# Query projections of latent attention: from one tile per head to one nope tile per pair and one rope tile per two pairs

## The chip, the cores and the metric

One core of a Trainium2 chip runs the whole program. The metric is the device time of one execution in microseconds, as the median of several runs. One more execution was taken by the profiler; its trace has the start and duration of every instruction.

## The reference, cut to what matters

One decoder layer: multi-head latent attention for 1024 prompt tokens and for 8 x 4 sample tokens (these with a paged cache of 4096 positions), then LayerNorm, a gated feed-forward part with a width-3 convolution, LayerNorm. The change touches the query projection and the rotation of queries and keys.

```python
d = x @ w_a_down
c_q = rms_norm(d[..., :384], g_q_norm)                 # Q_LORA
c_kv = rms_norm(d[..., 384:640], g_kv_norm)            # KV_LORA
k_r = d[..., 640:]                                     # 32 rotary columns, one key for all heads
q = (c_q @ w_a_uq).reshape(b, t, 16, 96)               # 16 heads, 64 plain + 32 rotary
x1, x2 = xf[..., :16], xf[..., 16:]                    # apply_rope
rope = concatenate([x1 * cos - x2 * sin, x1 * sin + x2 * cos])
sc = (einsum(q_nope, k_nope) + einsum(q_rope, k_r)) * ATTN_SCALE, causal
o = softmax(sc) @ v
```

## The kernel before, in words

All products are in float32 accuracy: each operand is split into a high part (a rounding to the engine's faster float32r) and a low part (the rest), and each product is three matmuls (hi x hi, hi x lo, lo x hi), `mm3`, lines 728 to 730. The splitting is the work of ScalarE (high, a copy) and VectorE (low, a subtraction).

Stages: `project` (down projection, norms, transposes; to about 98 us), `attend` (prompt attention, 98 to 503 us), `decode` (sample attention with the pages, to about 720 us), `mix`, `ffn`. The heads of `attend` are worked in 8 pairs p. A pair has 16 units n (a query group g of 256 tokens from the last to the first, head hh, half r); wide units come first (scores up to 1024 columns wide), narrow ones (128 to 512) at n = 8 to 15. For every n, TensorE issues in this order: the scores of n + 1, the transposes of the probabilities of n - 1, products with the values (`VALUES_AT`), and pieces of projection work. While pair p is worked on, the projections of pair p + 1 are done, at places written out by hand (`OWN_AT`, `NEXT_AT`): `wt` (a transposed weight), `v0`, `v1` (values), `k0`, `k1` (keys), six query units `q<head><chunk>` with three chunks of CH = 352 tokens, and `t0`, `t1`, `ql` of the pair itself.

The query of one head has 128 rows on the partitions: 64 plain, 32 rotary and 32 rotary with their halves exchanged. The exchange comes from copied weight columns (`split_hi`, on POOL). A table of constants (`rope_query_tab`: the scale, cos, and sin with its sign) is multiplied onto all 128 rows by VectorE (`q_scale`, L1003, tile `q_scaled`, called qf); the keys have the rotary key twice below the plain rows, so that the sum over rows gives x cos + x' sin. ScalarE then makes `q_hi` (`q_high`), VectorE `q_lo` (`q_low`). PSUM has 8 banks: 0 and 1, 2 and 3 hold scores in turn, 4 and 5 transposed probabilities, 6 the output, 7 and free score banks the projections (`BANK`).

Each engine does its instructions in program order. The conditions between them that the text needs:

- scores(n) wait for exp(n - 2) (semaphore `pr`), and for n = 0, 4, 8 for the queries' low parts (`ql_ok`);
- `row_max(n)` (VectorE, `neg_max`, L1018) waits for scores(n), exp(n) (ScalarE, `probs`, L897) for `row_max(n)` and for `inverse(n - 2)` (VectorE, `inv_sums` and `inv_rows`);
- `inverse(n)` waits for exp(n), and stands in VectorE's order behind the projection work of step n + 1;
- at the end of a pair the first scores of the next one wait for `q_scaled` of "q00", since it holds bank 3, and `t0` of the new pair waits for "q10" to leave bank 7.

```python
                    if n == 0 and p:
                        q_high(p, NEXT_AT[NU])
                    if n == 1 and p:
                        inv_copy(p - 1, 0)
```

Of the kernel before, what the change touches and what calls it, by code (L numbers as in the profile page):

```python
# [35 lines left out]
H = 16  # L36
# [54 lines left out]
def rope_tables():  # L91
# [9 lines left out]
    s2 = np.concatenate([-sin, sin], 1).T * np.float32(ATTN_SCALE)  # L101
    plain = np.full((NOPE, TOK), ATTN_SCALE, np.float32)
    query = np.stack([np.concatenate([plain, c2, s2], 0), np.concatenate([c2, s2, plain], 0)], 1)
# [19 lines left out]
def project(nc, io, m, sem):  # L123

    ps = m.ps
    with ExitStack() as ctx:
# [115 lines left out]
        def _(pe):  # L242
# [79 lines left out]
            def early(name):  # L322
# [8 lines left out]
                else:  # L331
                    pe.wait_ge(d_sq, TT - 1)
                    a, b, c, out, hh = m.w.q_halves, (m.cqhi, m.cqlo), slice(0, CH), o[:, 0:CH], int(name[1])
                    sides = [(a[0][:, k, hh, :], a[1][:, k, hh, :], b[0][:, k, c], b[1][:, k, c]) for k in range(KQ)]
# [29 lines left out]
            early("q00")  # L364
            early("q10")
# [76 lines left out]
        def _(dve):  # L442
# [18 lines left out]
            def n_lo_halves(i):  # L461
# [15 lines left out]
            def norm(i):  # L477
# [15 lines left out]
                for at in (DOWN - ROPE, DOWN):  # L493
                    nc.vector.tensor_tensor(nrm[0:r, b, at:at + 16], rt[0:r, 0, :], rt[0:r, 1, :], ALU.subtract)
                    last = nc.vector.tensor_tensor(nrm[0:r, b, at + 16:at + 32], rt[0:r, 2, :], rt[0:r, 3, :], ALU.add)
# [42 lines left out]
FIRST_BANK = {"v0": 0, "k0": 1, "q00": 4, "q10": 5, "wt": 6, "v1": 7, "k1": 2, "q02": 3, "q12": 0, "q01": 4, "q11": 5}  # L538
FIRST_AFTER = {"q12": "v0", "q01": "q00", "q11": "q10"}


class HeadWeights:


    LOADS = 5 * 16

    def __init__(self, tile, stage, sem):
# [7 lines left out]
        self.staged, self.swapped = sem("w_staged"), sem("w_swapped")  # L555
        self.hi_ok, self.lo_ok = sem("w_split_hi"), sem("w_split_lo")

    def load(self, sp, io, p):
        wq = io["w_a_uq"].rearrange("(k p) n -> p k n", p=P)
        for hh, to, n, at in ((0, 0, QK_HEAD, 0), (1, 0, ROPE, QK_HEAD + NOPE), (1, NOPE, NOPE, QK_HEAD)):  # L560
            c = p * 2 * QK_HEAD + at
            sp.dma_start(self.q_staged[:, :, hh, to:to + n], wq[:, :, c:c + n]).then_inc(self.staged, 16)
# [4 lines left out]
    def split_hi(self, nc, pool, p):  # L567

        pool.wait_ge(self.staged, (p + 1) * self.LOADS)
        half, q = ROPE // 2, self.q_staged  # L570
# [1908 lines left out]
```

## Time and profile before

| | us |
|---|---|
| median of 3 runs | 1630.54 (1629.57 to 1631.71) |
| profiled execution | 1627.18 |
| its span, first to last instruction | 1625.3 |
| TensorE busy | 1587.8 |
| VectorE busy | 931.9 |
| ScalarE busy | 586.3 |
| POOL busy | 194.8 |
| one pair of the attention, from the first scores of one (210.56) to those of the next (261.14) | 50.6 |

Busy times are sums of instructions' durations. Matmuls overlap each other in the array, so a matmul's duration (0.32 us for 352 columns) is about twice the distance from its start to the next one's; distances are to be read from starts in the timeline.

### The profile page before, as it was taken

How to read it: one execution, taken by the hardware profiler on the slowest of the kernel's cores; microseconds unless marked ns; L12 is line 12 of the kernel's file. 1: busy time of each engine (PE TensorE's matmuls, PEld its weight loads, DVE VectorE, ACT ScalarE, POOL GpSimd, SP SyncE). 2: the span in 40 equal slices, each digit the busy share in tenths (PEclk: the TensorE clock that was granted, in tenths of full speed). 3: DMA queues.
4: the chain of work that ended last, by engine and by line, in shares of the span. 5: the costliest groups of instructions: out<-in, count | busy, mean ns of one | idle time of the engine just before them, and what ended most of it. 6: DMA issues, size and time to landing. Idle time of an engine off the chain costs nothing. (4 is left out here: it accounts for less than half of the span.)

```text
span 1625.3 us, 29603 instructions
## 1 busy us (share of the span) xinstructions
PE 1587.8 (98%) x10341; PEld 1405.0 (86%) x10341; DVE 931.9 (57%) x1813; ACT 586.3 (36%) x1280; POOL 194.8 (12%) x305
## 2 busy tenths in 40 slices
PE   7989999999999999999999999999999999999997
PEld 6988888888886666657889999999999999999995
DVE  5565666656665555545665465544546455455556
ACT  5455655556553333322233131121312213121145
POOL 1000000000000430000003021120211202112001
PEclk9999999999999999999999999999999999999999
DMA  6111111011113765533123020220202201021003
GB/s 211 54 29 30 28 24 24 13 28 26 23 53 114 237 208 169 167 114 95 39 69 100 27 65 13 65 65 26 65 13 65 64 27 52 25 65 39 13 27 117
DMA packets 151135, 109.18 MB, mean 67 GB/s; under 512 B 54791, under 2 KB 139973, under 8 KB 150904
## 3 DMA queue, kind: packets, MB, share of 16 engines
q1 hardware_dynamic: 148488, 101.76, 21.4%
q0 software_dynamic: 1968, 5.59, 1.2%
q8 instruction: 56, 0.92, 0.2%
q10 hardware_dynamic: 576, 0.52, 0.1%
q14 instruction: 47, 0.39, 0.1%
HBM read 101.88 MB, written 10.14 MB: 69 GB/s over the span
## 5 line engine op out<-in xcount | busy, mean ns | idle before, releaser
L1905 PE MATMUL banks<-act_hi,up_hi 128*128 128x352 f32 (+2 forms) x1040 | 335.6, 323 | 0.7 <-PEq L1497 0.7
L1906 PE MATMUL banks<-act_lo,up_hi 128*128 128x352 f32 (+2 forms) x1040 | 335.1, 322 | 0.0
L1907 PE MATMUL banks<-act_hi,up_lo 128*128 128x352 f32 (+2 forms) x1040 | 334.9, 322 | 0.0
L1905 PEld LDWEIGHTS banks<-act_hi,up_hi 128*128 128x128 f32 x1040 | 195.5, 188 | 1.0 <-issue 0.9
L1906 PEld LDWEIGHTS banks<-act_lo,up_hi 128*128 128x128 f32 x1040 | 195.3, 188 | 0.0
L1907 PEld LDWEIGHTS banks<-act_hi,up_lo 128*128 128x128 f32 x1040 | 195.2, 188 | 0.0
L2204 DVE TENSOR_TENSOR o_t<-o_t,banks 128x352 f32<-128x352 f32 x240 | 120.9, 520 | 94.4 <-PE banks L1907 94.1
L2183 DVE SCALAR_TENSOR_TENSOR conv_out<-conv_in,conv_now,conv_out 128x1072 f32<-128x1072 f32 x42 | 63.9, 1520 | 185.8 <-ACT conv_out L2058 185.8
L1018 DVE TENSOR_REDUCE neg_max<-banks 128x1 f32<-128x896 f32 (+7 forms) x128 | 96.7, 756 | 116.8 <-PE banks L804 116.3
L2049 ACT ACTIVATE conv_in<-banks 128x352 f32<-128x352 f32 x84 | 36.3, 458 | 336.1 <-PE banks L1907 336.1
L1905 PE MATMUL banks<-gated_hi,down_hi 128*128 128x352 f32 x480 | 155.8, 325 | 0.0
L1906 PE MATMUL banks<-gated_lo,down_hi 128*128 128x352 f32 x480 | 154.2, 321 | 0.0
L1907 PE MATMUL banks<-gated_hi,down_lo 128*128 128x352 f32 x480 | 154.1, 321 | 0.0
L897 ACT ACTIVATE probs<-banks,neg_max 128x896 f32<-128x896 f32 (+7 forms) x128 | 94.6, 739 | 43.3 <-DVE inv_rows L1028 23.2
L1905 PEld LDWEIGHTS banks<-gated_hi,down_hi 128*128 128x128 f32 x480 | 90.1, 188 | 1.2
L1906 PEld LDWEIGHTS banks<-gated_lo,down_hi 128*128 128x128 f32 x480 | 90.2, 188 | 0.0
L1907 PEld LDWEIGHTS banks<-gated_hi,down_lo 128*128 128x128 f32 x480 | 90.1, 188 | 0.0
L815 PE MATMUL banks<-ident,probs 128*128 128x128 f32 x576 | 86.9, 276 | 2.5 <-DVE probs_t L1039 2.3
L728 PE MATMUL banks<-k_hi,q_hi 128*128 128x512 f32 (+2 forms) x192 | 71.9, 374 | 8.3 <-DVE q_scaled L1003 6.1
L833 PE MATMUL banks<-probs_t,v_rows 128*64 128x256 f32 (+1 forms) x640 | 72.8, 365 | 0.8 <-DVE probs_t L1039 0.8
L2186 DVE SCALAR_TENSOR_TENSOR conv_out<-conv_in,conv_now,conv_out 128x1072 f32<-128x1072 f32 x42 | 69.3, 1651 | 1.5
L815 PEld LDWEIGHTS banks<-ident,probs 128*128 128x128 f32 x576 | 62.0, 141 | 6.4 <-DVE probs_t L1039 4.3
(340 smaller groups left out, 3085.0 us busy)
## 6 DMA issues: line engine op xcount, KB each, us to landing
weight_stage<-in_w_f_up SPq DMA_DIRECT2D x44, 512.0 KB, 4.8
c_stage<-in_cache_kv_latent SPq DMA_DIRECT2D x140, 128.0 KB, 2.3
down_stage<-in_w_f_down SPq DMA_DIRECT2D x22, 512.0 KB, 4.3
head_weights_stage<-in_cache_kv_latent SPq DMA_DIRECT2D x56, 128.0 KB, 2.2
rope_query_tab<-in_cache_kv_latent SPq DMA_DIRECT2D x56, 128.0 KB, 2.2
o_t<-in_x_prompt SPq DMA_DIRECT2D x8, 512.0 KB, 3.8
rope_rows<-in_cache_k_rope SPq DMA_DIRECT2D x256, 16.0 KB, 2.0
wo_stage<-in_w_a_out POOLq DMA_DIRECT2D x8, 512.0 KB, 4.7
```

Source lines behind the costliest of these rows:

```text
L728: nc.tensor.matmul(o, ws[0], xs[0], start=first, stop=False)
L815: last = nc.tensor.transpose(ps[:, 4 + t % 2, k * P:(k + 1) * P], prob[:, n % 2, c + k * P:c + (k + 1) * P], m.ident[:, :])
L833: last = nc.tensor.matmul(ps[d, 6, q], v[:, j, d], pt[:, g % 2, hh, j, q], start=j == 0, stop=j == 2 * g + 1)
L897: nc.scalar.activation(prob[:, n % 2, 0:wd], src, ACT.Exp, bias=nmax[:, n % 2:n % 2 + 1], accum_out=sums[:, n % 2:n % 2 + 1]).then_inc(pr, 1)
L1018: nc.vector.tensor_reduce(nmax[:, n % 2:n % 2 + 1], src, axis=AXX, op=ALU.max, negate=True).then_inc(nm_ok, 1)
L1905: nc.tensor.matmul(o, ws[0], xs[0], start=first, stop=False)
L1906: nc.tensor.matmul(o, ws[0], xs[1], start=False, stop=False)
L1907: return nc.tensor.matmul(o, ws[1], xs[0], start=False, stop=last)
L2049: nc.scalar.activation(u[i][:, 2 + CH * c:2 + CH * c + CH], src, ACT.Copy).then_inc(ev, 1)
L2183: nc.vector.scalar_tensor_tensor(out=v[i][:, 0:CW], in0=u[i][:, 1:UW - 1], scalar=cwi[:, 1, i, j:j + 1], in1=v[i][:, 0:CW], op0=ALU.mult, ...
L2186: nc.vector.scalar_tensor_tensor(out=v[i][:, 0:CW], in0=u[i][:, 0:UW - 2], scalar=cwi[:, 0, i, j:j + 1], in1=v[i][:, 0:CW], op0=ALU.mult, ...
L2204: nc.vector.tensor_tensor(y, y, ps[:, 4 + unit % 4, 0:CH], ALU.add).then_inc(add, 1)
```

## The change

A pair now has three nope units `n<chunk>` (64 plain rows of both heads, 128 rows together). For every even pair there are also three rope units `r<chunk>` (32 rotary rows of four heads, those of this pair and the next). For an odd pair the rotary rows have been kept in SBUF (`q_raw`, 64 rows) by a ScalarE copy (`rope_saved`). The tile qf now holds both heads of one chunk, instead of two units in turn. ScalarE copies the plain rows out of PSUM with the scale; VectorE makes the rotary rows with four products of 32 rows (cos and sin for each head). The halves are exchanged on the key side: the second copy of the rotary key is written with exchanged halves in `norm`, so the weights need no copied columns, and the table has cos and sin for all rows. `q_high` and `q_low` take both heads at once. For the samples, the sum of the two rotary parts in `m.sr`, before by POOL, is now done with a permuting matmul (`swapped_rope`, last pair, n = 4) and four additions on VectorE (`rope_blocks`, n = 5).

```diff
-s2 = np.concatenate([-sin, sin], 1).T * ATTN_SCALE;  plain = full(ATTN_SCALE)
-query = np.stack([concatenate([plain, c2, s2], 0), concatenate([c2, s2, plain], 0)], 1)
+s2 = np.concatenate([sin, -sin], 1).T * ATTN_SCALE
+query = np.stack([np.tile(c2, (4, 1)), np.tile(s2, (4, 1))], 1)
...
-                    nc.vector.tensor_copy(m.rtnew[:, :], ps[0:2 * ROPE, 7, 3 * P:3 * P + N_SAMPLE])
+                    for b in range(2):
+                        nc.vector.tensor_copy(m.rtnew[b * ROPE:(b + 1) * ROPE, :], ps[0:ROPE, 7, 3 * P:3 * P + N_SAMPLE])
...
-                for at in (DOWN - ROPE, DOWN):
+                for at, swapped in ((DOWN - ROPE, 0), (DOWN, 16)):
...
     def load(self, sp, io, p):
-        for hh, to, n, at in ((0, 0, QK_HEAD, 0), (1, 0, ROPE, QK_HEAD + NOPE), (1, NOPE, NOPE, QK_HEAD)):
+        for h in range(2):
+            c = (2 * p + h) * QK_HEAD
+            sp.dma_start(self.q_staged[:, :, 0, h * NOPE:(h + 1) * NOPE], wq[:, :, c:c + NOPE]).then_inc(self.staged, 16)
+        for h in range(0 if p % 2 else 4):
+            c = (2 * p + h) * QK_HEAD + NOPE
+            sp.dma_start(self.q_staged[:, :, 1, h * ROPE:(h + 1) * ROPE], wq[:, :, c:c + ROPE]).then_inc(self.staged, 16)
     def split_hi(self, nc, pool, p):
-        for hh, rope in ((0, NOPE), (1, 0)):
-            for at, to in ((rope + half, rope + ROPE), (rope, rope + ROPE + half)):
-                last = nc.gpsimd.tensor_copy(q[:, :, hh, to:to + half], q[:, :, hh, at:at + half])
...
+CHUNKS = "210"
+EARLY = [["wt", "v0", "v1", "k1", "r2", "n2", "r1", "n1", "k0", "r0", "n0"], ["wt", "v0", "v1", "k1", "n2", "n1", "k0", "n0"]]
+FIRST = ["v0", "k0", "r0", "n0", "wt", "v1", "k1", "r2", "n2", "r1", "n1"]
-NEXT_AT = {4: "wt", 5: "v0", 6: "v1", 8: "k1", 9: "q02", 10: "q12", 11: "q01", 12: "q11", 14: "k0", 15: "q00", 16: "q10"}
+NEXT_AT = [{4: "wt", 5: "v0", 6: "v1", 8: "k1", 9: "r2", 10: "n2", 11: "r1", 12: "n1", 14: "k0", 15: "r0", 16: "n0"},
+           {4: "wt", 5: "v0", 6: "v1", 8: "k1", 10: "n2", 12: "n1", 14: "k0", 16: "n0"}]
+ROPE_AT = {10: "2", 12: "1", 16: "0"}
+NOPE_AT = {11: "2", 13: "1"}
+LOW_AT = {12: "2", 14: "1"}
...
 PE:  elif name == "t0":
-                    bank_free(p, "q10" if p else "v1")
+                    bank_free(p, "n0" if p else "v1")
 PE, scores:
-                if n == 0:
-                    pe.wait_ge(pj_dve, dve_count(p, "k0" if p else "q12"))
+                if n == 0 and p:
+                    bank_free(p, "k0")
+                if n == 1:
+                    bank_free(p, ("n1" if p % 2 else "r0") if p else "r2")
 PE, end of a pair:
-                    pe.wait_ge(pj_dve, dve_count(p + 1, "q00"))
                     scores(p + 1, 0)
...
 ACT:
+            def rope_saved(p, c):
+                act.wait_ge(pj, pj_count(p, "r" + c))
+                if p:
+                    act.wait_ge(rp_ok, chunk_at(p - 1, c) + 1)
+                copy(m.q_raw[:, CH * int(c):CH * int(c) + CH], ps[NOPE:P, proj_bank(p, "r" + c), 0:CH]).then_inc(pj_act, 1)
+            def q_nope(p, c):
+                act.wait_ge(pj, pj_count(p, "n" + c))
+                act.wait_ge(ql_ok, chunk_at(p, c))
+                for hh in range(2):
+                    r = slice(hh * NOPE, (hh + 1) * NOPE)
+                    last = nc.scalar.activation(qf[r, hh, :], ps[r, proj_bank(p, "n" + c), 0:CH], ACT.Copy, scale=ATTN_SCALE)
+                last.then_inc(pj_act, 1)
+            def q_high(p, c):
+                act.wait_ge(pj_act, act_count(p, "n" + c))
+                act.wait_ge(rp_ok, chunk_at(p, c) + 1)
+                if c == "2":     # six small copies of sample columns, then
+                copy(q_hi[:, :, CH * int(c):CH * int(c) + CH], qf[:, :, :]).then_inc(qh_ok, 1)
 ACT, step n:
                     if n == 0 and p:
-                        q_high(p, NEXT_AT[NU])
+                        q_nope(p, "0")
+                        q_high(p, "0")
+                    if more and n in NOPE_AT:
+                        q_nope(p + 1, NOPE_AT[n])
+                        q_high(p + 1, NOPE_AT[n])
+                    if more and p % 2 and n in ROPE_AT:
+                        rope_saved(p + 1, ROPE_AT[n])
...
 DVE:
+            def q_rope(p, c, heads=(0, 1)):
+                for hh in heads:
+                    for part in range(2):
+                        r = slice(hh * ROPE, (hh + 1) * ROPE)
+                        at = slice(NOPE * (p % 2) + hh * ROPE, NOPE * (p % 2) + (hh + 1) * ROPE)
+                        src = m.q_raw[r, cols] if p % 2 else ps[r, proj_bank(p, "r" + c), 0:CH]
+                        to = (NOPE, 0)[hh] + part * ROPE
+                        last = nc.vector.tensor_tensor(qf[to:to + ROPE, hh, :], src, tab[at, part, cols], ALU.mult)
+                if heads[-1]:
+                    last.then_inc(rp_ok, 1)
+            def q_low(p, c):
+                dve.wait_ge(qh_ok, chunk_at(p, c) + 1)
+                nc.vector.tensor_tensor(q_lo[:, :, cols], qf[:, :, :], f32(q_hi[:, :, cols]), sub).then_inc(ql_ok, 1)
 DVE, step n, behind row_max(p, n + 1):
+                    if n == 1 and p:
+                        q_low(p, "0")
+                    if more and n in LOW_AT:
+                        q_low(p + 1, LOW_AT[n])
+                    if more and n in ROPE_AT:
+                        q_rope(p + 1, ROPE_AT[n], (0,))
+                    if more and n in (9, 15):
+                        k_low(p + 1, NEXT_AT[0][n - 1])
                     if n:
                         inverse(p, n - 1)
                         pt_odd(p, n - 1)
+                    if more and n in ROPE_AT:
+                        q_rope(p + 1, ROPE_AT[n], (1,))
 DVE, before the first pair:
+            k_low(0, "k0")
+            q_rope(0, "0")
+            k_low(0, "k1")
+            q_low(0, "0")
+            q_rope(0, "2")
+            q_low(0, "2")
+            q_rope(0, "1")
+            q_low(0, "1")
             row_max(0, 0)
```

## Rows read from the trace of the kernel before

**Rows 1.** The page: span, and busy us of each engine (share of the span, instructions).
```profile
span 1625.3 us, 29603 instructions
PE 1587.8 (98%) x10341; PEld 1405.0 (86%) x10341; DVE 931.9 (57%) x1813; ACT 586.3 (36%) x1280; POOL 194.8 (12%) x305
```
**Rows 2.** Windows, 204 to 256 us: length, busy us by engine, granted clock, DMA.
```profile
204.00:256.00 52.00, 50.75 (x355) 42.61 (x352) 33.35 (x88) 29.53 (x73) 2.25 (x7) 1.00 0.12 23
```
**Rows 3.** Waits, 100 to 475 us: who waited for whom, total us, times, longest.
```profile
PE banks L728 <- DVE q_scaled L1003: 6.1, 7, 0.9
```
**Rows 4.** Timeline of PE at a pair boundary: start, duration, instruction, [idle before].
```profile
206.35 0.41 PE L728 MATMUL banks<-cq_hi,wq_hi 128*128 128x352 f32 x1
...
209.31 0.38 PE L815 MATMUL banks<-ident,probs 128*128 128x128 f32 x2
210.56 0.50 PE L728 MATMUL banks<-k_hi,q_hi 128*128 128x512 f32 x1 [0.87 <-DVE q_scaled L1003]
...
214.40 0.60 PE L775 MATMUL banks<-ident,v_t 128*128 128x128 f32 x4
```
**Rows 5.** Timeline of DVE at the same boundary.
```profile
207.81 0.68 DVE L995 TENSOR_TENSOR k_lo<-banks,k_hi 64x512 fp32r<-64x512 f32 x1 [2.54 <-ACT k_hi L887]
208.51 0.69 DVE L996 TENSOR_TENSOR k_lo<-banks,k_hi 64x512 fp32r<-64x512 f32 x1
...
210.00 0.94 DVE L1003 TENSOR_TENSOR q_scaled<-banks,rope_query_tab 128x352 f32<-128x352 f32 x2
210.86 0.15 DVE L1024 RECIPROCAL inv_sums<-sums 128x1 f32<-128x1 f32 x1
...
211.15 0.42 DVE L1039 COPY probs_t<-banks 128x256 f32<-128x256 f32 x1
212.16 1.09 DVE L1018 TENSOR_REDUCE neg_max<-banks 128x1 f32<-128x896 f32 x1 [0.59 <-PE banks L804]
```
**Rows 6.** Groups by line and shape: count, busy us, mean ns, idle before.
```profile
L583 DVE TENSOR_TENSOR wq_lo<-head_weights_stage,wq_hi 128x768 fp32r<-128x768 f32 x8 | 7.6, 946 | 0.0
...
L2049 ACT ACTIVATE conv_in<-banks 128x352 f32<-128x352 f32 x84 | 36.3, 458 | 336.1 <-PE banks L1907 336.1
...
L887 ACT ACTIVATE q_hi<-q_scaled 128x352 fp32r<-128x352 f32 x48 | 23.6, 494 | 34.7 <-DVE q_scaled L1003 34.5
...
L897 ACT ACTIVATE probs<-banks,neg_max 128x768 f32<-128x768 f32 x16 | 14.4, 899 | 0.5 <-DVE inv_rows L1028 0.5
```
**Rows 7.** Timeline of all engines in the narrow steps, 244 to 253 us.
```profile
244.42 0.69 DVE L1018 TENSOR_REDUCE neg_max<-banks 128x1 f32<-128x512 f32 x1 [1.78 <-PE banks L804]
...
245.02 0.51 DVE L1003 TENSOR_TENSOR q_scaled<-banks,rope_query_tab 128x352 f32<-128x352 f32 x1
...
245.57 0.47 ACT L887 ACTIVATE q_rope<-q_scaled 32x32 f32<-32x32 f32 x2
...
246.19 0.48 ACT L887 ACTIVATE q_hi<-q_scaled 128x352 fp32r<-128x352 f32 x1
...
252.90 0.38 PE L728 MATMUL banks<-k_hi,q_hi 128*128 128x256 f32 x1
```
**Rows 8.** Timeline of ACT at the boundary of rows 4.
```profile
213.28 1.01 ACT L897 ACTIVATE probs<-banks,neg_max 128x896 f32<-128x896 f32 x1 [2.18 <-DVE neg_max L1018]
...
214.28 0.49 ACT L887 ACTIVATE q_hi<-q_scaled 128x352 fp32r<-128x352 f32 x1
```
**Rows 9.** Timeline of all engines at the first pair, 106 to 114 us.
```profile
106.12 0.69 DVE L996 TENSOR_TENSOR k_lo<-banks,k_hi 64x512 fp32r<-64x512 f32 x1
...
110.40 0.47 PE L728 MATMUL banks<-k_hi,q_hi 128*128 128x512 f32 x1 [1.39 <-DVE q_lo L1009]
...
111.96 1.09 DVE L1018 TENSOR_REDUCE neg_max<-banks 128x1 f32<-128x896 f32 x1
...
113.09 1.01 ACT L897 ACTIVATE probs<-banks,neg_max 128x896 f32<-128x896 f32 x1 [0.37 <-DVE neg_max L1018]
```
**Rows 10.** Waits of SP's queue over the whole span.
```profile
SPq L690 <- PE banks L763: 67.5, 6, 16.3
```

More of the change, by code:

```diff
@@ L836, in values, with swapped_rope @@
                 last.then_inc(pv, 1)
+            def swapped_rope():
+                bank_free(PAIRS - 1, "ql")
+                pe.wait_ge(zr, 1)
+                pe.wait_ge(qh_ok, chunk_at(PAIRS - 1, "2") + 1)
+                nc.tensor.matmul(ps[0:ROPE, 7, :], swap[:, :], m.qr[:, 1, :, :].rearrange("r b c -> r (b c)"),
+                                 start=True, stop=True).then_inc(sw_ps, 1)
             def inverse_rows(p, g):
-                if g == 3:
-                    bank_free(*((p + 1, "v1") if p + 1 < PAIRS else (p, "ql")))
+                if g == 3 and p + 1 < PAIRS:
+                    bank_free(p + 1, "v1")
+                elif g == 3:
+                    pe.wait_ge(sr_ok, 1)
                 elif g == 2 and p + 1 < PAIRS:
@@ L956, in _ @@
             act.wait_ge(vch, 1)
-            for name in FIRST[:len(EARLY)]:
-                if name in BY_ACT:
+            for name in FIRST:
+                if name[0] == "k":
+                    k_hi(0, name)
+                elif name[0] == "r":
+                    rope_saved(0, name[1])
+                elif name[0] == "n":
+                    q_nope(0, name[1])
+                    q_high(0, name[1])
+                else:
                     take(0, name)
-                elif name[0] == "k":
-                    k_hi(0, name)
-                else:
-                    q_high(0, name)
             for p in range(PAIRS):
@@ L978, in _ @@
                         take(p, OWN_AT[n])
-                    if more and n in NEXT_AT and NEXT_AT[n] in BY_ACT:
-                        take(p + 1, NEXT_AT[n])
-                    if more and n - 1 in NEXT_AT and NEXT_AT[n - 1] in Q_UNITS:
-                        q_high(p + 1, NEXT_AT[n - 1])
-                    if more and n in NEXT_AT and NEXT_AT[n][0] == "k":
-                        k_hi(p + 1, NEXT_AT[n])
+                    unit = NEXT_AT[(p + 1) % 2].get(n, "") if more else ""
+                    if unit in ("wt", "v0", "v1"):
+                        take(p + 1, unit)
+                    if more and n in NOPE_AT:
[3 more added lines that the diff above has]
+                        rope_saved(p + 1, ROPE_AT[n])
+                    if unit in ("k0", "k1"):
+                        k_hi(p + 1, unit)
             inv_copy(PAIRS - 1, 0)
@@ L1006, in q_low @@
-            def q_low(p, name):
-                i, hh, c = place_in(p, name, Q_UNITS), int(name[1]), int(name[2]) * CH
-                dve.wait_ge(qh_ok, p * len(Q_UNITS) + i + 1)
-                nc.vector.tensor_tensor(q_lo[:, hh, c:c + CH], qf[:, i % 2, :], f32(q_hi[:, hh, c:c + CH]), sub).then_inc(ql_ok, 1)
+            def q_rope(p, c, heads=(0, 1)):
+                cols = slice(CH * int(c), CH * int(c) + CH)
+                if heads[0] == 0:
+                    if p % 2:
+                        dve.wait_ge(pj_act, act_count(p - 1, "r" + c))
+                    else:
+                        dve.wait_ge(pj, pj_count(p, "r" + c))
+                    if chunk_at(p, c):
+                        dve.wait_ge(ql_ok, chunk_at(p, c))
+                for hh in heads:
+                    for part in range(2):
+                        r = slice(hh * ROPE, (hh + 1) * ROPE)
[5 more added lines that the diff above has]
+                    last.then_inc(rp_ok, 1)
```

199 lines of the change are left out of this document (94 added, 105 removed).

## The prediction

> **What bounds the kernel now.** I read the page first: of a span of 1625.3 us TensorE is busy 98%, VectorE 57%, ScalarE 36% [rows 1]. Busy matmuls are pipelined, so 98% is not proof; the stage has to be looked at. The table of windows for 204 to 256 us, about one pair of heads of the prompt attention, shows 50.75 of 52 us on TensorE at a granted clock of 1.00, but only 33.35 on VectorE and 29.53 on ScalarE [rows 2]. The waits of 100 to 475 us, seven pair boundaries, show one TensorE wait that matters: 6.1 us in 7 pieces, on `q_scaled` [rows 3]. So before the change TensorE sets a pair's time, and the two other engines have slack on average. But one step of a pair is a ring, and the average hides it: scores need the exp of two steps before, that exp needs `inverse` (DVE) of two steps before, and both stand in program order behind whatever projection work the two engines have been given. The question is whether the ring stays shorter than TensorE's own work when TensorE loses work and the others gain it. I use the timelines for that.
>
> **What is removed.** Query units were 6 per pair, 48 in all; now there are 3 nope units per pair and 3 rope units for every second pair, 36. The 12 that go lie in the steps n = 9, 11 and 15 in which an odd pair (1, 3, 5, 7) is prepared. Two units run from 206.35 to 209.31 on TensorE, 1.48 us each [rows 4], so 12 x 1.48 = 17.8 us of TensorE work go.
>
> **What is added.** Per chunk of 352 columns, 24 chunks:
> - VectorE had two `q_scaled` (two in a row take 0.94, and the next instruction starts 0.86 behind the first [rows 5]) and two `q_lo`. Now it has four products on 32 rows each and one `q_lo` of 704. The number of rows doesn't shorten an instruction: the half-height `k_lo` of 512 takes 0.69. The successive products write different rows, as the two `k_lo` do; those start 0.70 apart with 0.68 of duration, so without overlap [rows 5]. Bounds for a pair of products: 0.86 (overlap, as in `q_scaled`) and 1.04 (none). I take 1.04, since `k_lo` is the nearer row. `q_lo` of 704: between the 0.51 of one product of 352 and the 0.946 of a subtraction of 768 [rows 6, 7], 0.87.
> - ScalarE had two `q_hi` (0.494). Now two scaled copies out of PSUM of 352 (as `conv_in`, 0.458 each, 0.92 together), one `q_hi` of 704, between 0.494 and the 0.899 of an exp of 768 [rows 6], 0.84, and for even pairs a copy of the other pair's rope rows, 0.46. The six small sample copies of chunk 2 now stand in a row before one `q_hi`: three take 0.62 (245.57 to 246.19 [rows 7]), so 1.24.
>
> By the Trainium skill (VectorE: DVE Perf Modes, section on two Vector instructions with no wait between them) an instruction that starts in another group of 32 partitions than its predecessor's is held until all earlier ones have finished. By that rule each of the four products is held, 1.04 for two; if the rule did not apply here, 0.86, and each ring below would be 0.2 to 0.4 us shorter. The `k_lo` rows [rows 5] agree with the rule; the `q_scaled` pair shows only the other case.
>
> **The pair boundary, 7 times.** Before: the last key unit ends at 206.35, `k_lo` at 208.51 + 0.69 = 209.20, and the two `q_scaled` start at 210.00 [rows 5]; TensorE's scores start at 210.56 after 0.87 of waiting and `t0` at 214.40 [rows 4]. TensorE's own work from the key unit to `t0` is 214.40 - 206.35 - 0.87 = 7.2 us. Now `t0` needs bank 7, and that bank (unit `n0`) is emptied by ScalarE's scaled copies, which stand behind the new pair's first exp. The ring: first two products 210.00 to 211.04; reciprocal to the end of the score copy, as before 210.86 to 211.57, 0.71: 211.75; second two products, which stand before `row_max` of the new pair: 212.79; `row_max` at 212.82 instead of 212.16; its exp 1.12 later (213.28 - 212.16 [rows 5, 8]): 213.94; ScalarE free 1.00 later (214.28 - 213.28 [rows 8]): 214.94; two scaled copies: 215.86; `t0` at 215.9, 1.5 us later than before, and everything behind it moves by that. It is the same for both parities, because `n0` and `r0` lie before it on TensorE and are covered. The wait of 0.87 disappears (scores now need only `k_lo`, 209.20) but comes back as waits ahead of the values and of `t0`. Behind `t0` the steps 1 to 8 keep their pace: 0 more. `split_lo` is 384 instead of 768 wide for an odd pair, about 0.35 less at a place where VectorE is late: -0.35.
>
> **The middle, n = 10 to 14.** With both rope and nope units (even pair prepared) `row_max(11)` starts at 244.42. From it: 0.60 to 245.02 [rows 7]; products 1.04; `inverse(9)` 0.39; exp(11) 0.86; copy of scores 0.40; scaled copies 0.92; small copies 1.24; `q_hi` 0.84; `q_lo("2")`, which VectorE waits for in order, 0.92; the first products of chunk 1 1.04; `inverse(11)` 0.39; exp(13) 0.63; then scores(15): 9.3 us, at 253.75. Before they were at 252.90 [rows 7]: +0.85. TensorE's own work over the same stretch is about 8.5 us (252.90 - 244.42). With an odd pair prepared, the ring starts about 1.6 earlier (unit r2 is gone, and scores(11) no longer drag) and is as long: 252.15, so -0.75; the other two removed units, 2.96 us, bring nothing, for TensorE waits for exp(12), exp(13) and `inverse(11)`.
>
> Sum: three even pairs 3 x (1.5 + 0.85) = 7.1; four odd ones 4 x (1.5 - 0.75 - 0.35) = 1.6.
>
> **The first pair.** Scores start at 110.40 after `q_lo`, `row_max` at 111.96, exp at 113.09 [rows 9]. Now ScalarE has about 1.5 us more before `k_hi("k1")`, so `k_lo("k1")` ends at 106.12 + 0.69 + 1.5 = 108.3 instead of 106.8 [rows 9]. Then in order, with hops: `q_lo` 0.87; four products 2.08; small copies and `q_hi` 2.08; `q_lo` 0.87 (scores start, 114.3); four products 2.08; `q_hi` 0.84; `q_lo` 0.87: `row_max` at 118.15, +6.2. Lower end: products overlap and the 1.5 is hidden, +4; upper end +8, if more of the ScalarE copies are exposed.
>
> **Edits with no cost.** Key halves are written swapped: same instructions. The rope key of the samples takes one more copy, the gain loads none. The weight loads of an even pair are 8 DMAs instead of 5, of an odd pair 4; SP's queue, in which they stand ahead of 32 page loads, waits 67.5 us for TensorE at this point in 6 pieces [rows 10], so it has the time; with that cover gone the page loads behind them would be late, and nothing reads those before the decode stage. POOL's four swap copies go, and nothing waits for POOL. The sum of the rope blocks moves from POOL to one matmul and four products of 256 columns on VectorE in the last pair (0.5 as the 512 wide score matmul [rows 4], and 4 x 0.42 = 1.7 as the copy of 256 [rows 5]), where VectorE has a gap at n = 6; bounds 0 and +1.7, taken 0.
>
> Total: 7.1 + 1.6 + 6.2 = 14.9, rounded down to 14.5 since hops are counted fully. The profiled execution took 1627.18 (span 1625.3 [rows 1]); that becomes 1641.7. The median of the runs shown lies 3.4 above the profiled execution, 1630.54, which gives **1645 us**.
>
> **Rivals.**
> - *TensorE stays the bound* (the other side). Place: the seven boundaries and the middles; the rings would have to be shorter than TensorE's own 7.2 (even) and 5.7 us (odd), against 9.55 worked out. Eight units in the middles give 11.8, an odd boundary 1.3 (scores can't start before `k_lo`, 209.2), an even one 0.87: 11.8 + 5.2 + 2.6 = 19.6, 1611 us. For it: averages of 33 and 30 of 52 us. Against: the order of instructions.
> - *Only the boundary ring counts*, the middle one is covered: odd pairs 1.5 - 2.96 - 0.35 = -1.8, even +1.5, first pair +4: 4 x -1.8 + 3 x 1.5 + 4 = +1.3, 1632. It decides if small copies and `q_hi` overlap so that the middle ring is below 7 us. Spread 1625 to 1637.
> - *Slower still*: rings as above plus the upper ends (rope blocks 1.7, first pair +8, half a microsecond more per pair): +22, 1653. For it: each hop between engines that I took at 0.05 may cost 0.2.
> - That the change doesn't remove the units is excluded by the lists of units in the diff.
>
> **Numbers.** Forecast 0.60, its own range 1638 to 1652; TensorE the bound 0.12; boundary only 0.18 (0.08 faster, 0.06 the same, 0.04 slower); slower still 0.10. Within 0.2% (3.3 us) is about what a measurement can't tell from no change. Faster 0.20, same 0.06, slower 0.74. The range 1620 to 1653 leaves out TensorE as the bound and half of the last case.
>
> **What would show it.** The waits of TensorE in the attention grow from about 10 to over 30 us, on ScalarE's scaled copies ahead of `t0` (about 2.4 and 3.8 us per boundary), on exp and `inverse` ahead of scores(14), (15). The pair period, 50.6 us now, becomes about 51 and 53 in turn. The products should start 0.52 apart. Wrong it would be if pairs take 47 us for odd preparation, if `t0` doesn't wait, or if VectorE's `q_lo("2")` doesn't wait for `q_hi`.

## The result, and the profile after

The changed kernel takes 1663.27 us, median of 5 runs (1661.66 to 1664.86); the kernel before took 1630.54 beside it. The ratio is 1.0198, 95% interval 1.0186 to 1.021: 32.7 us slower, where the forecast said 14.5 slower and its range ended at 1653. The direction held and the size did not.

The page, as in [rows 1]:

```profile
span 1661.5 us, 29467 instructions
PE 1589.3 (96%) x10235; PEld 1396.6 (84%) x10235; DVE 965.6 (58%) x1842; ACT 607.2 (37%) x1316; POOL 185.7 (11%) x271
```

TensorE has 106 matmuls fewer in the records and is busy 1.5 us longer. At half clock a matmul shows a longer duration (the 16 below, 3.22 us against 1.74), so the busy row already holds a hint. The largest waits of TensorE in the attention part, 95 to 530 us, stand below (who waited for whom, total us, times, longest). Before, over the same window, the largest was the 6.1 of [rows 3], and all waits that the profile lists came to 16.0; now they come to 47.6:

```profile
PE banks L802 <- ACT q_scaled L991: 10.4, 7, 1.6
PE banks L865 <- issue: 7.8, 7, 1.2
PE banks L892 <- DVE inv_rows L1118: 7.6, 7, 1.7
PE banks L751 <- DVE q_lo L1088: 5.6, 1, 5.6
PE banks L865 <- DVE o_t L1135: 4.1, 7, 0.6
PE banks L751 <- ACT probs L940: 3.9, 12, 0.7
```

The first is `t0`, once per boundary; the second the value matmuls just ahead of it ("issue" is a wait for which the profile shows no releaser); the third the transpose of the inverse sums in the narrow steps; the fourth the first pair; the fifth, the value matmuls waiting for an *output* product, was in no step of the prediction.

The profiled spans differ by 36.2 us, the medians by 32.7; the section on e11 and e12 comes back to this. To place the 36.2, take the start of `t0` as the clock of the pairs. Before: 113.26, then every 50.6 us up to 467.38. After: 122.84, 175.59, 230.01, 284.05, 338.81, 393.24, 447.64, 501.75.

| part | before | after | more by | forecast |
|---|---|---|---|---|
| start of the attention part | 98.52 | 101.71 | 3.2 | 0 |
| from there to `t0` of the first pair | 14.74 | 21.13 | 6.4 | 6.2 |
| three periods in which an even pair is prepared | 151.8 | 163.6 | 11.8 | 7.1 |
| four periods in which an odd pair is prepared | 202.3 | 215.3 | 13.0 | 1.6 |
| last pair, and the stages behind it | 1157.9 | 1159.8 | 1.9 | 0 |

The periods were to be about 51 and 53 us in turn. They are 52.75, 54.04, 54.43 and 54.11 with an odd pair prepared, and 54.42, 54.76 and 54.40 with an even one.

**The boundary went as forecast.** TensorE at the boundary of 230 us (start, duration, instruction, idle before), which answers to [rows 4]:

```profile
223.39 0.48 PE L751 MATMUL banks<-k_hi,q_hi 128*128 128x512 f32 x1
...
225.91 0.87 PE L865 MATMUL banks<-probs_t,v_rows 128*64 128x256 f32 x8 [0.99 <-issue]
227.03 0.47 PE L751 MATMUL banks<-k_hi,q_hi 128*128 128x512 f32 x1 [0.25 <-DVE q_scaled L1081]
...
230.01 0.66 PE L802 MATMUL banks<-ident,v_t 128*128 128x128 f32 x4 [1.29 <-ACT q_scaled L991]
```

VectorE there, as in [rows 5]:

```profile
222.42 0.69 DVE L1063 TENSOR_TENSOR k_lo<-banks,k_hi 64x512 fp32r<-64x512 f32 x1
...
223.57 0.42 DVE L1135 TENSOR_TENSOR o_t<-banks,inv_t 128x256 f32<-128x256 f32 x1
224.03 1.05 DVE L1081 TENSOR_TENSOR q_scaled<-banks,rope_query_tab 32x352 f32<-32x352 f32 x2
...
225.84 1.04 DVE L1081 TENSOR_TENSOR q_scaled<-banks,rope_query_tab 32x352 f32<-32x352 f32 x2
226.92 1.09 DVE L1108 TENSOR_REDUCE neg_max<-banks 128x1 f32<-128x896 f32 x1
```

And ScalarE, as in [rows 8]:

```profile
228.04 1.01 ACT L940 ACTIVATE probs<-banks,neg_max 128x896 f32<-128x896 f32 x1 [5.11 <-DVE neg_max L1108]
228.95 0.19 ACT L940 ACTIVATION_READ_ACCUMULATOR probs<-banks,neg_max 128x1 f32 x1
229.04 0.91 ACT L991 ACTIVATE q_scaled<-banks 64x352 f32<-64x352 f32 x2
```

Read the three along the ring: second products to 226.88, `row_max` at 226.92, its exp at 228.04 (1.12 later, the figure used), scaled copies at 229.04 for 0.91, `t0` at 230.01. From the end of the last key unit to `t0` it is 9.77 us here and 9.87 at an odd boundary, against 8.08 before: 1.7 and 1.8 more, forecast 1.5.

**The narrow steps did not.** TensorE in the narrow steps of the period from 230.01, in which an odd pair is prepared:

```profile
265.32 0.33 PE L751 MATMUL banks<-k_hi,q_hi 128*128 128x128 f32 x1 [0.45 <-ACT probs L940]
267.41 0.41 PE L892 MATMUL banks<-ident,inv_rows 128*128 128x128 f32 x2 [1.29 <-DVE inv_rows L1118]
268.00 0.39 PE L751 MATMUL banks<-k_hi,q_hi 128*128 128x256 f32 x1 [0.18 <-ACT probs L940]
269.54 3.22 PE L865 MATMUL banks<-probs_t,v_rows 128*64 128x256 f32 x16 [0.63 <-DVE o_t L1135]
```

and VectorE over the same stretch:

```profile
264.82 0.89 DVE L1088 TENSOR_TENSOR q_lo<-q_scaled,q_hi 128x704 fp32r<-128x704 f32 x1 [1.35 <-ACT q_hi L930]
265.81 1.05 DVE L1081 TENSOR_TENSOR q_scaled<-q_rope,rope_query_tab 32x352 f32<-32x352 f32 x2
...
267.89 1.05 DVE L1081 TENSOR_TENSOR q_scaled<-q_rope,rope_query_tab 32x352 f32<-32x352 f32 x2
268.97 0.42 DVE L1135 TENSOR_TENSOR o_t<-banks,inv_t 128x256 f32<-128x256 f32 x1
```

Two things stand here that no step had. Bank 6 takes the values of group 1 only when `o_done(2)` (L1135, step 13 by `OUT_AT`) has read group 2 out of it, and that stands in VectorE's order behind all the products of chunk 1: TensorE waits for it in all seven periods, 0.63 in six of them and 0.35 in one. And the 16 value matmuls behind it take 3.22 us here, where the same 16 take 1.7 elsewhere. The windows give the clock (length, busy us by engine, then the granted clock, DMA share, GB/s):

```profile
262.00:266.00 4.00, 3.55 (x28) 3.00 (x24) 2.37 (x7) 3.13 (x11) 0.00 (x0) 1.00 0.11 16
266.00:270.00 4.00, 1.90 (x12) 1.21 (x13) 3.83 (x12) 1.24 (x5) 0.00 (x0) 0.90 0.11 17
270.00:274.00 4.00, 4.00 (x22) 2.67 (x19) 1.72 (x5) 1.92 (x5) 0.00 (x0) 0.68 0.11 16
```

After waits of 0.45, 1.29, 0.18 and 0.63 us within 5 us TensorE runs at the lower of its two levels for about 3 us and loses 1.5. It happens in three of the four periods that prepare an odd pair (3.22, 3.26, 2.84 us for the 16; in the first they take 1.74 behind nearly the same waits, 0.41, 1.29, 0.18 and 0.63), and in none of the others. From scores(10) to the transposes of the probabilities of unit 14, TensorE needed 17.5 us before (17.6 once). Now it needs 19.44, 19.79 and 19.43 with an even pair prepared; with an odd pair, 17.90 in the period at full clock, and 19.37, 19.76 and 19.49 in the three with half clock.

### The profile page after: what moved, and what is told of

Same layout as the page of the kernel before. It is cut to its first block and busy times, and to the rows that moved or that the text cites. A ratio compares the mean times of both kernels' runs of the same rounds, so it can differ in the third digit from the quotient of the medians.

```text
span 1661.5 us, 29467 instructions
## 1 busy us (share of the span) xinstructions
PE 1589.3 (96%) x10235; PEld 1396.6 (84%) x10235; DVE 965.6 (58%) x1842; ACT 607.2 (37%) x1316; POOL 185.7 (11%) x271
## 5 line engine op out<-in xcount | busy, mean ns | idle before, releaser
L865 PE MATMUL banks<-probs_t,v_rows 128*64 128x256 f32 (+1 forms) x640 | 77.0, 380 | 12.7 <-issue 7.8
L865 PEld LDWEIGHTS banks<-probs_t,v_rows 128*64 128x64 f32 x640 | 45.8, 142 | 37.3 <-issue 22.0
```

Source lines behind the costliest of these rows:

```text
L865: last = nc.tensor.matmul(ps[d, 6, q], v[:, j, d], pt[:, g % 2, hh, j, q], start=j == 0, stop=j == 2 * g + 1)
```

## The experiments

The theory going in: the time is set by rings through VectorE and ScalarE, so TensorE's removed 17.8 us are worth nothing; what the rings cost is the products' number, the copies of `n0` behind the first exp, `o_done(2)`, and half clock behind stalls. Rivals stand with each run. The kernels start from the changed kernel unless said otherwise.

**e1: the 12 removed units put back as dead work.** TensorE computes the rope unit again in steps 9, 11 and 15 of the periods that prepare an odd pair, into a bank nobody reads then.

```diff
+                    if p + 1 < PAIRS and p % 2 == 0 and n in (9, 11, 15):
+                        refill(p + 1, n)     # KQ x mm3 of the rope part, read by no one
```

> The changed kernel, but TensorE computes the rope unit for odd pairs too, at its old places n = 9, 11 and 15, into banks that nobody reads: the 12 units (12 x 1.48 = 17.8 us of TensorE work) are back, nothing on ScalarE or VectorE is different, and the result is the same. Theory (the rings through ScalarE and VectorE set a pair's time): the changed kernel's pairs take 54.0 us with an odd pair prepared and 54.4 with an even one, so the odd ones become 54.4: +1.6 us in all, about 1665, and less if the half-speed stretches go. Rival (TensorE's amount of work counts): +17.8, about 1681.

1667.5 us (4 runs), ratio 1.0221 (1.0204 to 1.0238): 4.2 us over the changed kernel for 17.8 us of work. Six steady periods took 326.6 us against 326.2; most of the rest came in the first period (55.76 against 52.75), where the clock of 100 to 200 us was 0.93 against 0.95. So in the changed kernel most of TensorE's removed work does not set the period, and "TensorE stays the bound" is out. The work is not quite free, though. In e1 the 16 value matmuls take 1.73 or 1.74 in three of the four odd periods, at a clock of 1.00 from 200 to 500 us, against one of four in the changed kernel (3.12 in the first period of e1). Periods without a half-clock stretch that prepare an odd pair take 54.1 to 54.6 in e1, and 52.75 in the changed kernel (52.61 in e5, whose attention code is the same). At full clock the 4.4 us of work per period thus cost 1.3 to 2.0, and the half clock, which comes in most periods without that work, hides it.

**e2: two products of 64 rows in place of four of 32.** The sine part is left out: each head is multiplied once.

```diff
-                    for part in range(2):
-                        ... tensor_tensor(qf[to:to + ROPE, hh, :], src, tab[at, part, cols], ALU.mult)
+                    ... tensor_tensor(qf[to:to + NOPE, hh, :], src, tab[at, hh, cols], ALU.mult)
```

> Timing only: the four VectorE products of 32 rows per chunk become two of 64 rows (one per head, with one table for both parts), which leaves the sine part of the rotation wrong. Theory: two instructions less in the boundary ring (one before inverse(15), one before the new pair's row_max, 1.05 us together) and two in the middle ring (1.05 us), o_done(2) 0.5 earlier, so 2.1 to 2.8 us per pair, 15 to 20 in 7 pairs, and 2 to 4 in the first pair: 1640 to 1646 us. Rival (ScalarE's extra copies alone make the wait): under 5 us.

1640.15 us, ratio 1.0055 (1.0038 to 1.0071): 48 products fewer give back 23.1 us. From the groups by shape (count, busy us, mean ns), first the changed kernel, then e2:

```profile
L1081 DVE TENSOR_TENSOR q_scaled<-banks,rope_query_tab 32x352 f32<-32x352 f32 x48 | 24.8, 517 | 1.4
```

```profile
L1079 DVE TENSOR_TENSOR q_scaled<-banks,rope_query_tab 64x352 f32<-64x352 f32 x24 | 12.3, 513 | 0.8
```

A product costs 0.51 whether it has 32 or 64 rows. The 48 that go are 24.8 us of VectorE in an engine busy 58%, and nearly as much shows in the time: that is what lying on a ring means. Not all of the 23.1 is the products themselves. The wait for `o_done(2)` (4.1 in all) is gone from the list, and so are the three half-clock stretches (4.1 in all; the clock from 200 to 500 us is 1.00).

**e3: `q_nope` of chunk 0 copied before the new pair's first exp.**

```diff
                     if n == 0 and p:
-                        q_nope(p, "0")
                         q_high(p, "0")
...
+                    if more and n == NU:
+                        q_nope(p + 1, "0")
```

> One edit on ScalarE: the two scaled copies of unit n0 stand at the end of the old pair, before the first exp of the new pair, not behind it. Theory: t0 no longer waits (1.3 to 1.6 us, 7 times) and the next wait is that of scores(2) for the exp, which comes at its old place: about 1.2 us per boundary, 8 to 9 us in all, 1654 to 1655. Rival (the wait of t0 is only where a late VectorE shows, and row_max holds TensorE up just as long): no change, 1663.

1656.47 us, ratio 1.0149 (1.0132 to 1.0166): 6.8 less. The wait of `t0` is gone from the list, but scores and the values at the start of the boundary still wait as before; less came back than the 10.4 us that `t0` had waited. The half clock now comes in all four odd periods (2.98, 2.91, 2.60 and 2.79 for the 16 value matmuls). What is late next is the exp: the scores behind `t0` (283.00 in e3's trace) now wait 0.33 for it.

**e4: `o_done(2)` one step earlier.**

```diff
-OUT_AT = {9: 3, 13: 2, 16: 1}
+OUT_AT = {9: 3, 12: 2, 16: 1}
```

> One edit on VectorE: the division of group 2 (o_done) is issued at n = 12, before the products of the rope rows, not at n = 13 behind them. Theory: the values of group 1 no longer wait for it (0.63 us, 7 times) nor does the copy of the inverses on ScalarE, and the half-speed stretch behind that wait in odd pairs (1.5 us in 3 pairs) shortens: 4 to 9 us, 1654 to 1659. Rival: the ring is set by k0's way alone and the time is the same, 1663.

1655.87 us, ratio 1.0152 (1.0135 to 1.0169): 7.4 less. TensorE in e4 at the same place of the same pair:

```profile
266.52 0.41 PE L892 MATMUL banks<-ident,inv_rows 128*128 128x128 f32 x2 [1.29 <-DVE inv_rows L1118]
267.11 0.39 PE L751 MATMUL banks<-k_hi,q_hi 128*128 128x256 f32 x1 [0.18 <-ACT probs L940]
267.96 1.74 PE L865 MATMUL banks<-probs_t,v_rows 128*64 128x256 f32 x16
```

The wait of 0.63 is gone, and so is the half clock in this execution: 1.74 for the 16, at a clock of 1.00 from 200 to 500 us. Seven waits (4.1 in all) and three stretches (1.5, 1.5 and 1.1) are 8.2; 7.4 came back. This is the larger part of what the forecast missed in the odd periods (now 51.9 us at steady pace, against 54.0 to 54.4). That the missing 0.63 is what keeps the clock up is not shown: e10 below has the same edit and the half clock in two odd periods.

**e5: the first pair's weight loads behind the fourth token tile's load.**

```diff
-            m.w.load(sp, io, 0)
...
+                if i == 0:
+                    m.w.load(sp, io, 0)
```

> One edit on SP's queue: the eight weight DMAs of pair 0 are issued behind the load of the fourth token tile, not behind the third. Theory (the attention starts 3.2 us later, at 101.7 instead of 98.5, because four DMAs of 128-byte rows take 5.9 us of SP's queue and keep the weights and tokens of the first stage back): the first transpose of the attention comes at about 98.5 and the time falls by 3, to 1660. Rival (the late start is chance, or comes from the key's exchanged halves): 101.7 and 1663.

1663.33 us, ratio 1.0192 (1.0173 to 1.021), attention start 101.68: no change; taken up again in e8.

**e6: all four products behind `inverse` and the score copy.**

```diff
-                    if more and n in ROPE_AT:
-                        q_rope(p + 1, ROPE_AT[n], (0,))
...
-                        q_rope(p + 1, ROPE_AT[n], (1,))
+                        q_rope(p + 1, ROPE_AT[n])
```

> One edit on VectorE: in the steps 10, 12 and 16 all four products of a rope chunk stand behind inverse and the score copy, where two stood in front. No work is less. Theory: exp(11) and exp(13), which wait for inverse(9) and inverse(11), come 1.05 us earlier each; the products end at the same time as before. One of the two lies on the ring to scores(15) fully, the other in part, since the scaled copies wait for the products' end: 0.5 to 1.5 us per pair, 4 to 10 us in all, 1653 to 1659. Rival (the number of VectorE instructions counts, not their place): no change, 1663.

1664.41 us, ratio 1.0191 (1.0161 to 1.0222): nothing gained. TensorE in e6, odd pair prepared:

```profile
271.69 3.26 PE L865 MATMUL banks<-probs_t,v_rows 128*64 128x256 f32 x16 [1.69 <-DVE o_t L1135]
...
287.25 0.85 PE L802 MATMUL banks<-ident,v_t 128*128 128x128 f32 x4 [2.69 <-ACT q_scaled L991]
```

The wait for `inverse` became a wait of 1.69 for `o_done(2)`, which now stands behind four products, with half clock behind it in two of the four odd periods, and `row_max` of the new pair, still behind the products, makes `t0` wait 2.69. The same 2.1 us of products were pushed in front of the next consumer.

**e7: all reorderings together.** e3, e4, e5 and e6, and besides: in the first pair `row_max(0, 0)` ahead of the products of chunk 1; for odd pairs `row_max` of the new pair ahead of the boundary's products; the six small copies behind exp(12), with chunk 1's products waiting for them.

```diff
                     if more and n in ROPE_AT:
+                        if n == NU and p % 2 == 0:
+                            row_max(p + 1, 0)
                         q_rope(p + 1, ROPE_AT[n])
...
+                    if more and n == 12:
+                        samples(p + 1)
```

> The changed kernel with the same work in another order: the edits of the early n0 copies, of o_done at n = 12, of the late weight load and of the products behind inverse; for odd pairs the new pair's row_max in front of the boundary's products; the six small sample copies behind exp(12), with the products of chunk 1 waiting for them; in the first pair row_max in front of chunk 1. Theory (waits put there by program order, 33 us against the kernel before, or about 50 against TensorE's own work): 20 to 35 us of them go, 1628 to 1643 us. Rival (the added 27 us on VectorE and 22 on ScalarE cost the same wherever they stand): above 1645.

1625.85 us, ratio 0.9963 (0.9949 to 0.9977): faster than both kernels and than the 1628 to 1643 expected, with every unit, product and copy of the changed kernel.

**e8 to e10: the start, and which edits of e7 carry it.** e8 is the changed kernel with the weight loads behind the sixth tile's load and their split on VectorE two tiles later; e9 is e7 with the loads as in e8; e10 is e9 without its three last edits (products behind, `row_max` first, small copies later).

```diff
-            m.w.load(sp, io, 0)
...
+                if i == 2:
+                    m.w.load(sp, io, 0)
...
-                if i == 3:
+                if i == 5:
                     m.w.split_lo(nc, dve, 0)
```

> The changed kernel with the weight loads of the first pair issued behind the load of the sixth token tile (some 43 us into the run, where the DMA share is low) and their split on VectorE two tiles later; nothing else moves. Theory (contention): the four rope loads with their 128-byte rows fill the DMA engines while the fourth token tile is on its way, TensorE waits for that tile and then runs at half clock; e5 only moved the same collision by one tile. Then the transposes of the fourth tile start as in the kernel before or sooner (24.95 us or less), the attention part starts at 97.5 to 98.7 us instead of 101.7, and the time is 1659.5 to 1661. Rival (the 3.2 us come from something in the projections or in the order of the units, not from the loads): the attention part still starts at 101 to 102 us and the time is 1662.5 to 1664.

> e7 with the weight loads placed as in e8. If the loads are the cause of the late start, e7's 1625.9 us fall by about 3 to 1622 to 1623.5; if they are not, 1625 to 1627.

> e9 without its last three edits: all four products stand ahead of the inverse again, the first row maximum of the next pair is again behind the products, and the small sample copies are again ahead of the scaled ones. Theory (the parts hide one another: moving the products alone gave nothing, since the values then waited for the earlier output copy, but once the output copy is a step earlier the boundary chain of products, row maximum and exponential is what is left): these three edits are worth 15 to 22 us together, so this kernel takes 1639 to 1645. Rival (each edit is worth what it measured alone, the products' place nothing): this kernel takes within 4 us of e9, and the sum of the single gains (6.8, 7.4 and about 3 for the loads and 2 for the first pair, from 1663.3) would have to be found elsewhere.

e8: 1662.89 us, ratio 1.0198 (1.0183 to 1.0213), attention start 102.15. e9: 1625.0, ratio 0.9963 (0.995 to 0.9977), start 100.37. The expected 3 us came in neither time (0.4 less than the changed kernel, 0.9 less than e7), so the theory behind e5 and e8 fell. e10: 1648.84, ratio 1.0109 (1.0089 to 1.0129), 4 above what was expected of it: e3 and e4 alone add up to 14.2 (1649.1), so the new order of the first pair adds nothing that shows. The three last edits are then worth 23.8 us in e9, while the first of them alone was worth nothing in e6; no run separates the three. The periods say where (odd prepared, even prepared, at steady pace): e10 50.4 and 52.7, e9 47.0 and 51.5, 17 us in seven periods. Most of the rest is half clock in the first and the last odd period of e10, which take 53.12 and 52.15. Its first, on TensorE, without any wait for `o_done(2)`:

```profile
158.82 0.66 PE L893 MATMUL banks<-ident,inv_rows 128*128 128x128 f32 x2 [1.29 <-DVE inv_rows L1123]
160.90 3.26 PE L866 MATMUL banks<-probs_t,v_rows 128*64 128x256 f32 x16
```

In e9 all value matmuls of group 1 take 1.73 or 1.74. In e9, at a boundary, VectorE and then TensorE:

```profile
215.08 2.11 DVE L1095 TENSOR_TENSOR q_scaled<-banks,rope_query_tab 32x352 f32<-32x352 f32 x4
217.22 1.09 DVE L1122 TENSOR_REDUCE neg_max<-banks 128x1 f32<-128x896 f32 x1
```

```profile
217.33 0.47 PE L752 MATMUL banks<-k_hi,q_hi 128*128 128x512 f32 x1 [1.28 <-DVE q_scaled L1095]
218.86 0.60 PE L803 MATMUL banks<-ident,v_t 128*128 128x128 f32 x4
```

`t0` doesn't wait any more; the even boundary keeps one wait of 1.28 for the four products, since scores(1) overwrite bank 3, out of which they read the rope unit. With an odd pair prepared, the products read SBUF and no listed wait of TensorE is for them; such a period is 3.6 us shorter than before (50.6, now 47.0), for 4.4 us of removed units. No run puts the units back into this order, so how much of the 3.6 is theirs is not shown. An even period stays 0.9 longer than before. The seven periods are 11.7 shorter than those of the kernel before, and the way from the start of the attention part to `t0` is 5.4 longer (20.14 against 14.74).

**e11 and e12: is the late start the change's?** e11 is the kernel before with its query loads cut into six DMAs, four of them of short rows; e12 is the kernel before, profiled once more.

```diff
-        for hh, to, n, at in ((0, 0, QK_HEAD, 0), (1, 0, ROPE, QK_HEAD + NOPE), (1, NOPE, NOPE, QK_HEAD)):
+        for hh, to, n, at in ((0, 0, NOPE, 0), (0, NOPE, half, NOPE), (0, NOPE + half, half, NOPE + half),
+                              (1, 0, half, QK_HEAD + NOPE), (1, half, half, QK_HEAD + NOPE + half), (1, NOPE, NOPE, QK_HEAD)):
```

> The kernel before, with only its query weight loads cut as finely as in the changed kernel: the rope columns of a pair come in four DMAs of 16 columns (as many rows as the four rope loads of the changed kernel, half as wide), for every pair, 8 DMAs instead of 5. Same data, same units, same order elsewhere. Theory (the number of short rows in the queue costs the projection stage its start): the attention part starts at 101 to 102 us instead of 98.5 and the time is 1633 to 1634.5, 0.2% over the kernel before. Rival (the start wanders by itself: with the same projection code the last two kernels started at 102.2 and 100.4): no shift beyond that scatter, 1629.5 to 1632, and a start between 98 and 102 with TensorE at half clock in some slice between 12 and 32 us if it is late.

> The kernel before, unchanged, profiled once more, for the start of its attention part. If 98.5 us and a full clock between 12 and 32 us belong to the kernel, they come again within 0.3 us; if they belong to the one execution profiled so far, the start can be as late as 101 to 102 us, with half clock behind the wait for the fourth token tile, and the span longer by as much.

e11: 1632.12 us, ratio 1.0006 (0.9997 to 1.0015), start 101.25. e12: start 97.62, span 1626.0. TensorE's first transposes of the fourth token tile, in this order: before, e12, the changed kernel, e11.

```profile
24.95 1.09 PE L256 MATMUL banks<-ident,o_t 128*128 128x128 f32 x8 [3.50 <-DMA o_t<-in_x_prompt]
```

```profile
24.05 1.09 PE L256 MATMUL banks<-ident,o_t 128*128 128x128 f32 x8 [2.93 <-DMA o_t<-in_x_prompt]
```

```profile
26.56 1.74 PE L255 MATMUL banks<-ident,o_t 128*128 128x128 f32 x8 [2.76 <-DMA o_t<-in_x_prompt]
```

```profile
26.38 1.97 PE L256 MATMUL banks<-ident,o_t 128*128 128x128 f32 x8 [4.44 <-DMA o_t<-in_x_prompt]
```

Eight transposes take 1.09 at the upper level and 1.74 to 1.97 when part or all of them run at the lower one (1.97 in each of e1 to e8). The two profiles of the kernel before come back at full clock. The others, whatever their loads, do not (e10, with 1.28, comes nearest), and run on partly at half clock: from 26 to 30 us the granted clock is 1.00 before and in e12, 0.60 in the changed kernel, 0.50 in e8, 0.64 in e10. The late tile and the half clock together make the 3.2 us: the next small transposes of the sample tokens start at 29.67 before and at 32.86 in the changed kernel, already 3.19 later.

Whether the 3.2 us belong to the change is another matter. e11 starts 2.7 later than the kernel before in its profile and is only 1.1 slower in the median, at most 2.4 by its interval. Both profiled executions of the kernel before (1627.18 and 1627.79) are quicker than all but one of its 44 other executions on record (median 1631.4), while the changed kernel's profiled execution is its median. That is why the spans differ by 3.5 us more than the medians. It speaks for a late start in most executions of the kernel before too, but none of those was profiled, so this is not shown. With the same late loads e8, e9 and e10 start at 102.15, 100.37 and 99.78. Why the tile is late in e8 and e9, which have fewer transfers ahead of it than the kernel before, stays open.

## Why the prediction was right in direction and wrong in size

**Bound by rings, not by TensorE: right in the main.** e1 shows it (17.8 us of work for 4.2), e2 from the other side (24.8 us of VectorE for 23.1). At full clock the removed work is worth 1.3 to 2.0 of its 4.4 us per odd period. The forecast had the odd periods 1.95 shorter than the even ones, and at full clock they are 1.7 to 2.0 shorter (52.75 against 54.40 to 54.76); the half clock takes most of that back.

**Price of the parts: right.** Products 1.05 a pair and about 0.52 apart, forecast 1.04; the rule that was weighed (the Trainium skill, VectorE: DVE Perf Modes, section on two Vector instructions with no wait between them) agrees with the trace: the products start in other partitions than their predecessors and don't overlap. `q_lo` of 704 wide 0.89 against 0.87, two scaled copies 0.91 against 0.92, `q_hi` 0.79 against 0.84.

**Boundary, +1.5 in seven: right**, measured 1.7 to 1.8; TensorE's waits there are 2.5 and 3.7 us a boundary, forecast 2.4 and 3.8.

**First pair, +6.2: right**, 6.4 to `t0`, 6.7 to the first `row_max` and its exp. The second key unit's low part is 1.5 later, as forecast (111.50 against 106.81, from starts that lie 3.19 apart). TensorE waits 5.64 in one piece for `q_lo`, then starts at half clock:

```profile
117.91 0.77 PE L751 MATMUL banks<-k_hi,q_hi 128*128 128x512 f32 x1 [5.64 <-DVE q_lo L1088]
```

**The middle with an odd pair prepared, -0.75: wrong, the main miss.** The step that failed is "so -0.75", which let the period follow scores(15). scores(15) did come earlier, but by 0.3 in three periods and not at all in one. Behind it the values of group 1 wait for `o_done(2)` behind the products (0.63), and in three of the four periods TensorE then runs at half clock (1.5, 1.5 and 1.1). The stretch measures 17.90 at full clock and 19.37 to 19.76 with half clock, against 17.5: +0.4 once and +1.9 to +2.3 three times. The boundary adds 0.3 more than forecast, and the -0.35 for `split_lo` came only in part (0 to 0.25). The four periods are +3.3 each on average instead of +0.4: 11.4 us missed. e4 undoes the wait with one digit and gives back 7.4; in its profile the half clock is gone too. The wait is shown as a cause by e4. The half clock is measured where it stands, but why one execution of the same order has it and another not (e4 and e10) stays open.

**The middle with an even pair prepared, +0.85: mis-sized.** scores(15) was 1.23 to 1.5 later, and up to 0.7 more came behind it, `o_done(2)` again: 1.9 to 2.1. The three periods are 11.8 instead of 7.1, 4.7 us missed: 3 x 1.1 or a little more here, 3 x 0.2 at the boundary, and about 0.8 that no wait placed. Together 16.1, the difference between the 24.8 measured in the seven periods and the 8.7 forecast.

**Edits with no cost: taken at 0, and 1.9 measured from the last pair on.** 0 to 1.7 had stood for the rope blocks. No run separates them, and two profiles of the kernel before differ by 1.5 over this part (1157.9 and 1159.4). **The start is open**: 3.2 in the profile, 0 to 2.4 by e11, nothing by e8 and e9.

**The rivals.** "Slower still" had the right sign of the miss and the wrong place: dearer hops, half a microsecond more per pair. Hops at the boundary cost what was counted, within 0.3; what was missing was a wait for a buffer and the clock. "TensorE stays the bound" was priced at 1611; even e9, the fastest order that was run, gets to 1625. "Only the boundary ring counts" is out, since the middle grew in all seven periods, by 0.4 to 2.3.

## What to carry to other kernels

Work that is taken from the busiest engine pays only where the chain through the others is shorter than what is left; e9 shows that the same work in another order turns 2% slower into 0.4% faster. When an instruction is put into an in-order queue, list every consumer behind it up to the point where the stage ends, buffer releases (`o_done`) too, and not only the ring that was late before: here moving the products alone gave 0, and moving them together with the row maximum and the small copies, once the release was early, gave 24 us. A stall of TensorE can have a second price, the matmuls that run at half clock behind it, and this decides small margins.

## What the hardware showed that was not expected

- Half clock does not need one long wait, and the same order of instructions does not always bring it. 2.6 us of idle in four pieces within 5 us was followed by about 3 us at the lower level, at a cost of 1.5 us (16 matmuls 3.22 instead of 1.7). Executions of the same attention code (the changed kernel, e5, e8) had it in 3, 3 and 4 of the four odd periods. Without the piece of 0.63 the other three were followed by it in none of four in e4 and in two of four in e10 (3.26 and 2.96). With 4.4 us more work in these steps (e1) it came in one of four.
- A load can hold SP's queue for several times its usual time, and it isn't the short rows that do it. The four loads with 128-byte rows took 5.94 us together at the start and 2.32 in e8 some 21 us later. Over all 16 such loads of the changed kernel the median is 0.49 us and the longest 2.43; for the 16 with 256-byte rows the median is 0.48 and the longest 1.13, and in the kernel before one load of 512-byte rows took 2.26 at 8.80 us. The DMA engines are full at the start (share 1.09 from 8.5 to 14.5 us), but they were nearly so in e5 (0.91, 6.71 us for the four) and in e8 (0.85, 2.32), so what holds a load stays open. First the changed kernel, then e8:

```profile
7.39 1.07 SPq L568 DMA_DIRECT2D head_weights_stage<-in_w_a_uq  x2
8.51 5.94 SPq L571 DMA_DIRECT2D head_weights_stage<-in_w_a_uq  x4
```

```profile
29.46 2.32 SPq L572 DMA_DIRECT2D head_weights_stage<-in_w_a_uq  x4
```

- Three profiles of kernels with the same projection code (e8, e9, e10) start the next stage at 102.15, 100.37 and 99.78 us: a stage that waits on a full DMA system can scatter by more than the difference that is being looked for, and one profile is no measure of it.
